# The first attention's result: scaled by ScalarE, squared by GpSimd, four units' squares summed by VectorE in one pass

## The reference, cut to what matters

```
def diff_attend(q, k, v, lam):
    s = jnp.einsum('bqhcd,bkhcd->bhcqk', q, k, preferred_element_type=jnp.float32) * ATTN_SCALE
    p = jax.nn.softmax(s, axis=-1)
    a = p[:, :, 0] - lam * p[:, :, 1]
    return jnp.einsum('bhqk,bkhe->bqhe', a.astype(v.dtype), v)

def merge_heads(o, f, subln_g, fourier_w, w_out, lambda_init):
    B, T = o.shape[:2]
    o = (rmsnorm(o, subln_g) * (1.0 - lambda_init)).reshape(B, T, DIFF_WIDTH)
    return jnp.concatenate([o, fourier_groups(f, fourier_w)], axis=-1) @ w_out
```

## Time and profile before

| | |
|---|---|
| median of 3 runs | 1661.75 us (1661.38 to 1663.48) |
| the profiled execution, its own time | 1661.93 us |
| its span | 1660.6 us |
| PE busy | 1634.2 us, 98% of the span |
| DVE busy | 1128.0 us, 68% |
| ACT busy | 817.9 us, 49% |
| POOL busy | 241.3 us, 15% |
| the 12 units and the three pairs | from about 130 to 188 us |

### The profile page before, as it was taken

The page is one execution under the profiler, slowest core; times in us unless marked ns, Lnnn a source line. Parts: engine busy times, 40 slices in busy tenths (PEclk is TensorE's granted clock), DMA queues, the critical chain, the costliest instruction groups (busy, mean ns, idle before and its releaser), DMA issues.

```text
span 1660.6 us, 20917 instructions
## 1 busy us (share of the span) xinstructions
PE 1634.2 (98%) x7912; PEld 1318.7 (79%) x7912; DVE 1128.0 (68%) x1350; ACT 817.9 (49%) x1014; POOL 241.3 (15%) x380
## 2 busy tenths in 40 slices
PE   6999999999999999999999999999999999999999
PEld 3776788887778888788888878888888888888887
DVE  2898778897776764756558776664666568865653
ACT  3426654435565443644446554453544447564442
POOL 0001000000002240123203002240032203002240
PEclk9999999999999999999999999999999999999999
DMA  9686188897538876577655328675676654348660
GB/s 351 233 295 215 51 302 281 308 362 253 203 116 269 271 248 204 177 220 229 216 164 170 127 91 246 210 232 180 204 215 221 215 177 154 102 131 241 207 226 26
DMA packets 250292, 346.46 MB, mean 209 GB/s; under 512 B 16160, under 2 KB 197124, under 8 KB 250192
## 3 DMA queue, kind: packets, MB, share of 16 engines
q1 hardware_dynamic: 236016, 321.95, 58.7%
q0 software_dynamic: 11472, 17.34, 4.4%
q10 hardware_dynamic: 2704, 5.82, 1.0%
HBM read 329.58 MB, written 1.05 MB: 199 GB/s over the span
## 4 chain that ended last, share of the span: by engine, by line
PE 90%; DVE 6%; ACT 2%; issue 1%; DMA 1%; SPq 0%; DVEq 0%
PE bank L473 20%; PE bank L475 19%; PE bank L474 19%; PE bank L843 7%; PE bank L848 7%; PE bank L844 7%; DVE lo L1964 1%; PE bank L823 1%; PE bank L1353 1%; PE bank L1354 1%; PE bank L1356 1%; PE bank L1160 1%; PE bank L499 1%; DMA raw<-in_ada_w 1%; DVE ST L2261 1%
## 5 line engine op out<-in xcount | busy, mean ns | idle before, releaser
L1964 DVE TENSOR_TENSOR lo<-raw,hi 128x2048 fp32r<-128x2048 f32 x246 | 563.6, 2295 | 286.8 <-ACT hi L1405 286.5
L1405 ACT ACTIVATE hi<-raw 128x2048 fp32r<-128x2048 f32 x258 | 492.6, 1913 | 315.4 <-PE bank L475 171.5
L473 PE MATMUL bank<-hi,XTh 128*128 128x512 f32 (+1 forms) x1424 | 559.3, 393 | 4.9 <-DVE XTl L2075 4.5
L475 PE MATMUL bank<-hi,XTl 128*128 128x512 f32 (+1 forms) x1424 | 552.1, 388 | 0.0
L474 PE MATMUL bank<-lo,XTh 128*128 128x512 f32 (+1 forms) x1424 | 551.6, 387 | 0.0
L473 PEld LDWEIGHTS bank<-hi,XTh 128*128 128x128 f32 x1424 | 267.7, 188 | 68.4 <-issue 14.1
L475 PEld LDWEIGHTS bank<-hi,XTl 128*128 128x128 f32 x1424 | 267.7, 188 | 55.5
L474 PEld LDWEIGHTS bank<-lo,XTh 128*128 128x128 f32 x1424 | 267.9, 188 | 53.7 <-issue 1.0
L2927 POOL DMA_DIRECT2D HTR<-BLK x320 | 193.0, 611 | 723.2 <-DVE BLK L2461 680.2
L843 PE MATMUL bank<-hi,HTh 128*128 128x512 f32 x528 | 206.4, 391 | 0.0
L844 PE MATMUL bank<-lo,HTh 128*128 128x512 f32 x528 | 205.5, 389 | 0.0
(11 more groups left out here) (370 smaller groups left out, 1405.5 us busy)
## 6 DMA issues: line engine op xcount, KB each, us to landing
raw<-in_ffn_w_in SPq DMA_DIRECT2D x176, 512.0 KB, 4.9
raw<-in_ffn_w SPq DMA_DIRECT2D x132, 512.0 KB, 4.8
raw<-in_ada_w SPq DMA_DIRECT2D x96, 512.0 KB, 5.2
raw<-in_ffn_w_out SPq DMA_DIRECT2D x88, 512.0 KB, 4.1
raw<-in_w_mix_in SPq DMA_DIRECT2D x52, 512.0 KB, 4.6
raw<-in_od_pw_w SPq DMA_DIRECT2D x24, 512.0 KB, 5.5
HTR<-BLK POOLq DMA_DIRECT2D x240, 48.0 KB, 4.0
raw<-in_ev_w_in SPq DMA_DIRECT2D x20, 512.0 KB, 9.3
```

The lines of the kernel that those rows point to most:

```text
L473: pe.matmul(dst, xh, wh, start=start, stop=False)
L475: return pe.matmul(dst, xl, wh, start=False, stop=stop)
L1405: act.activation(hi[r][:, :], raw[g % RAW][:, :], ACT.Copy).then_inc(*up("hi", d))
L1964: dve.tensor_tensor(lo[r][:, :], raw[g % RAW][:, :], hi[r][:, :].bitcast(F32), ALU.subtract).then_inc(*up("lo", d))
```

## The change

The scaling of a unit's result leaves DVE. ACT now does it, straight from bank 3, as a copy with the reciprocal as its scale. GpSimd squares the result into its place in a larger OSQ. DVE adds up the squares of four units (two heads, both halves of the tokens) in one reduction, `pair_sum`. ACT's squares, with their sums, are gone. The place of ACT's step in its list moves too: it stands before the copy of unit u, no longer behind it.

```
-                act.wait_ge(*at("diff_out", u))
-                if u >= 1:
-                    act.wait_ge(*at("diff_sq", u - 1))
-                act.activation(OSQ[:, :], OROW[:, t, h * P:(h + 1) * P], ACT.Square,
-                               accum_out=SS[:, t, h:h + 1]).then_inc(*up("diff_sq", u))
+                act.wait_ge(*at("diff_valued", u))
+                act.wait_ge(*at("diff_inv", u))
+                act.activation(OROW[:, t, h * P:(h + 1) * P], bank[3][:, 0:P], ACT.Copy,
+                               scale=INV2[:, 2 * (u % 4):2 * (u % 4) + 1]).then_inc(*up("diff_out", u))
...
-                act.wait_ge(*at("diff_sq", 4 * (i + n) - 1))
+                act.wait_ge(*at("diff_sum", i + n - 1))
...
                 if u + 1 < N:
                     diff_softmax(u + 1)
+                if u >= 2:
+                    diff_values(u - 2)
                 if u == N - 2:
                     pair_norm(0, 2)
                 diff_turn(u)
...
                     four(u)
-                if u >= 2:
-                    diff_values(u - 2)
...
-                if u >= 2:
-                    diff_values(u - 2)
                 dve.wait_ge(*at("diff_inv", u))
...
-            def diff_values(u):
-                h, t = units[u]
-                dve.wait_ge(*at("diff_valued", u))
-                dve.tensor_scalar(OROW[:, t, h * P:(h + 1) * P], bank[3][:, 0:P], INV2[:, 2 * (u % 4):2 * (u % 4) + 1], None,
-                                  ALU.mult).then_inc(*up("diff_out", u))
+            def pair_sum(i):
+
+                dve.wait_ge(*at("diff_sq", 4 * i + 3))
+                dve.tensor_reduce(SS[:, :, 2 * i:2 * i + 2], OSQ[:, :, :, :], AX.X, ALU.add).then_inc(*up("diff_sum", i))
...
+                if u in (6, 10):
+                    pair_sum((u - 6) // 4)
...
+            for u in range(HEADS1 * T):
+                h, t = u // T, u % T
+                part = OROW[:, t, h * P:(h + 1) * P]
+                pool.wait_ge(*at("diff_out", u))
+                if u % 4 == 0 and u:
+                    pool.wait_ge(*at("diff_sum", u // 4 - 1))
+                pool.tensor_tensor(OSQ[:, t, h % 2, :], part, part, ALU.mult).then_inc(*up("diff_sq", u))
             pool.wait_ge(*at("o_full", 3))
```

More of the change, by code:

```diff
@@ L61 @@
     "row_scales": "rstd_in rstd rstd2",
-    "diff_scales": "diff_rstd diff_normed",
+    "diff_scales": "diff_rstd diff_normed diff_sum",
     "diff_statistics": "diff_max diff_inv diff_rel diff_mixed",
@@ L75 @@
     "down_parts": "down_bias down_gated",
-    "hg_decays": "hg_dec hg_tail",
+    "hg_decays": "hg_dec hg_tail diff_sq",
     "row_squares": "sq sq2 sq_in std std2",
     "exponents": "lam_exp lb_exp fox_zrow",
-    "diff_squares": "diff_sq diff_std",
+    "diff_squares": "diff_std",
     "hg_logs": "hg_e hg_ln hg_sig hg_z",
@@ L366, in program @@
         WB = tile_at("WB", [P, 2, P], ht_at + 28672)
-        OSQ = tile_at("OSQ", [P, P], ht_at + 29696)
+        OSQ = tile_at("OSQ", [P, T, 2, P], ht_at + 29696)
         U1 = tile_at("U1", [P, 2, 2 * S], ht_at + 32768)
@@ L2334, in vector_engine @@
             pair_norm(0, 0)
-            diff_values(N - 2)
             pair_norm(1, 0)
             pair_full(0, bank[6])
-            diff_values(N - 1)
             o_low(0)
+            pair_sum(2)
             pair_roots(2, 1)
```

## The result

The changed kernel takes 1665.15 us (median of 20 runs, 1664.24 to 1667.24) against 1661.73 us before (20 runs, 1660.73 to 1663.53). The ratio is 1.0022, with a 95% interval of 1.0016 to 1.0028: 3.4 us slower. The forecast was 1663.5, in a range of 1660.8 to 1666.0, with 0.13 for slower by over 0.2%. The range holds the time, but the loss is twice the forecast one. The profiled execution took 1665.22 us, its span is 1663.9.

The account below looks back on a forecast made before the run. The prediction took PE to bound the kernel, with DVE and PE setting the loop's time by turns. Holds of 1.8 and 0.8 less 0.5 and 0.4 given back made 1.7 us slower: 1663.5 us, range 1660.8 to 1666.0.

Parts of the forecast that it names:

- PE bounds, and what PE loses is handed on: Chain runs 90% through PE; a microsecond PE wins or loses in the attention reaches the kernel's end.
- the first hold: PE's values of unit 1 wait for ACT's scaling of unit 0, behind unit 3's exponentials, to free bank 3: 1.8 us late.
- the second hold: PE's values of unit 2 wait for ACT's scaling of unit 1, behind unit 4's late exponentials: another 0.8 us.
- what is given back: 0.5 us from DVE's spare time before unit 6's maxima, 0.4 from three later, shorter PE waits for the mixture.
- The 0.12 saved per unit: DVE's factor starts 0.20 us behind the reciprocal, not 0.32, without the scaling; counts only where PE waits for the mixture.
- what was called covered: DVE's first two sums fall in waits; the third adds 1.2 us in the tail, within 1.9 us of room.
- the sum is 1.8 + 0.8 - 0.5 - 0.4: Two PE holds less what is given back: 1.7 us slower at the end of the loop.
- The chance for slower by over 0.2%: 0.13 for over 3.3 us slower, from the GpSimd case and a third of the second rival.
- the second and third rival: ACT late in every later turn, some 1665, chance 0.16; GpSimd's squares holding DVE, 1666.7, chance 0.08.
- The hold comes back every turn: ACT's scaling 0.2 us late in each of eight turns from 4 on: 3.3 us slower, some 1665; chance 0.16.
- GpSimd holds VectorE: Squares of 0.40 us delay DVE's mixtures; all eight from unit 4 on give 4.9 us slower, 1666.7; chance 0.08.

Follow-up runs that it names:

- The runs with early scalings: Changed kernel with ScalarE's scalings of unit 0, units 0 and 1, or every unit put behind the next unit's copy AT: 1662.76, 1660.43 (again 1662.09), 1662.38 us.
- One early: Changed kernel with only unit 0's scaling put directly behind the copy AT of unit 1: 1662.76 us, ratio 1.0002.
- two early: Changed kernel with the scalings of units 0 and 1 put directly behind the copies AT of units 1 and 2: 1660.43 us; again, 1662.09 us.
- busy hold: Changed kernel with 7 idle products on TensorE ahead of unit 1's values, where it otherwise waits for OROW: 1664.2 us, ratio 1.0012.
- the two with the extra gate product: Changed kernel, without and with 7 idle products in the first wait, each repeating a gate product once more in the convolution's tail: 1664.65 and 1663.50 us.
- hold alone: Kernel before with one added wait: TensorE's values of unit 1 also wait for ScalarE's copy AT of unit 2: 1665.62 us, ratio 1.0021.

## Why the forecast was right and where it fell short

- **Right: PE bounds, and what PE loses is handed on.** The third pair's turning is 3.43 us late, and the medians differ by 3.4.
- **Right: the first hold.** Forecast PE's values at 148.77, 1.8 late; measured 148.83, 1.94 late by the fixed step. The runs with early scalings show that it comes from the scaling's place, and the hold put into the kernel before, that one wait costs its length (2.15 by the profile).
- **Right: the second hold.** 0.8 forecast, a wait of 0.73 measured, 0.89 with the hand-over. One early against two early prices it at 0.45 net.
- **Half right: what is given back.** 0.5 and 0.4 forecast, 0.50 and 0.65 measured. The 0.12 saved per unit was 0.13 (factor 0.19 behind the reciprocal). But of the three waits it was counted for, the first gave nothing (the transposes of unit 6 are 4.14 late, those of unit 5 4.08) and the other two 0.12 each. The other 0.44 came at units 10 and 11, where VectorE no longer waits for PE before it mixes. That 0.4 came out near 0.65 is in part luck.
- **Right: what was called covered.** The first two sums stand where VectorE waited anyway, the third ends in time: the second pair's split is at 187.88, and PE turned the third pair at 189.05 and reads the split behind that. The early runs show no cost of these.
- **The step that failed** is "the sum is 1.8 + 0.8 - 0.5 - 0.4". It took a wait on TensorE to cost its own length. The term that lacks is the clock behind it: 1.75 us between the values of unit 1 and the scores of unit 5 in the profile, 1.67 by the spans of the changed kernel and of the busy hold (44.10 and 42.43), 1.66 by the spans of the two with the extra gate product (44.07 and 42.41), 1.15 by the medians of these. The medians' number is smaller, and not because the fall lacks in some executions, since ten of the 11 runs have it. The two profiled executions are only 0.80 apart (1664.63 and 1663.83), because the one with the filling reached the scores of unit 4 0.90 us later (145.30 against 144.40). Whether the medians are closer for the same reason isn't known. Everything else came out at 1.76. The forecast doesn't speak of the clock; the earlier trace rows show it full before, and the sum took it to stay so. The chance for slower by over 0.2% should have carried this case.
- **Luck in the range.** It holds 1665.15 because its upper part was there for the second and third rival. The second stood at some 1665 and the time came out there, but for another reason: only two waits for OROW are listed, and none of 0.2 in each later turn.
- **The rivals.** "The hold comes back every turn" held a little: the values of units 4 and 7 start some 0.17 and 0.14 us behind where their transposes let them go. "GpSimd holds VectorE" needs the squares at another hour; where it happened, it was worth 0.05 or 0.06 a square, once 0.17.

What stays open: what decides whether the clock falls behind a wait of 1.9 us. Two executions with the wait of the same length differ in it, and at 460 us the clock fell in four of the ten profiles with the wait of 1.2 us, and not in the six others. How often it falls behind the hold put into the kernel before is open too. Two-early was not measured often enough to say that it wins.

## What to carry to other kernels

When a step moves to another engine, its duration matters less than what stands ahead of it in that engine's list. Look for the one buffer whose release the step signals, and ask for each turn, the odd first ones above all, when the new engine gets to it. If that puts a wait of nearly 2 us on TensorE (1.90 here), count the products behind it at half speed as well, as a case with a chance of its own. And when the clock falls in some executions only, compare spans between two fixed steps in the profiles, since medians mix both kinds.

## What the runs showed of the hardware

- TensorE's clock fell to half after a wait of 1.90 us and stayed there for 3.5 us of unbroken work (granted 0.51), at a price of 1.66 to 1.75 us. In an execution with 1.92 us of waiting at nearly the same place it stayed full (hold alone). Behind the wait of 0.73 us it stayed full in every profile here. The Trainium skill (TensorE: Matmul & The Clock Gate, HAM oscillation) describes this pattern, a wait between bursts of matmuls that throttles the clock so that the next burst starts slow. The changed kernel's trace agrees (0.51); that of the hold alone, with its clock of 1.00, shows that it need not come.
- 1.8 us of idle products in place of the wait kept the clock full, although nothing used them: granted 1.00 in all three profiles with such products. With the extra gate product, ten of 11 runs have a mean clock of 0.999 with the filling and ten of 11 have 0.998 without it.
- The kernel before has such a place too. At 460 us, after waits of 1.22 or 1.23 and of 0.57 us, the clock fell in four of the profiled executions (granted 0.83 in 460 to 470 us), which cost 1.6 us each time. Of the 99 runs of the kernel before beside the experiments, 31 took over 1663 us with a mean clock of 0.998, the others about 1661.5. That they are this same fall is inferred from the clock and the price; its own profiles don't have it.
- GpSimd's square makes VectorE's mixture beside it longer by far less than the square lasts: 0.05 or 0.06 us in most turns, 0.17 at most, of 0.40.
